# Prompt attention of a decoder trunk: quads of heads visited in pairs instead of one after another

## What is computed

```python
def sparse_attend(q, k_sel, v_sel, valid):
    s = jnp.einsum('bqhd,bqkhd->bqhk', q, k_sel, ...) * (DSA_HEAD_DIM ** -0.5)
    s = jnp.where(valid[:, :, None, :], s, -jnp.inf)
    p = jax.nn.softmax(s, axis=-1)
    return jnp.einsum('bqhk,bqkhd->bqhd', p.astype(v_sel.dtype), v_sel)
...
def dsa_out(o, g, w_out):
    return (o.reshape(B, L, DSA_WIDTH) * jax.nn.silu(g)) @ w_out
```

## Time and profile before

| | |
|---|---|
| median of 3 executions | 1161.84 us (1157.28 to 1166.62) |
| profiled execution, its own time | 1161.64 us |
| its span on the core | 1159.9 us, 25599 instructions |
| PE busy | 1120.7 us (97%), 10579 matmuls |
| PE weight loads | 979.1 us (84%) |
| DVE busy | 675.2 us (58%) |
| ACT busy | 493.8 us (43%) |
| POOL busy | 381.4 us (33%) |
| mean granted TensorE clock | 0.994 |
| prompt attention, first scores to output projection | 579.96 to 678.25 us |

### The profile page before, as it was taken

The page is one execution under the profiler, slowest core; times in us unless marked ns, Lnnn a source line. Parts: engine busy times, 40 slices in busy tenths (PEclk is TensorE's granted clock), DMA queues, the critical chain, the costliest instruction groups (busy, mean ns, idle before and its releaser), DMA issues. The chain is left out here.

```text
span 1159.9 us, 25599 instructions
## 1 busy us (share of the span) xinstructions
PE 1120.7 (97%) x10579; PEld 979.1 (84%) x10579; DVE 675.2 (58%) x1215; ACT 493.8 (43%) x968; POOL 381.4 (33%) x321
## 2 busy tenths in 40 slices
PE   8999999899999999999999899999999999999897
PEld 6889888899758988879945389999999889888796
DVE  6462255854999789677354546596444362245742
ACT  6542366643433321222353444322453451467643
POOL 5534213243313422114300124353344235312330
PEclk9999999999999999999999999999999999999998
DMA  5335233333315787784699932233220335233212
GB/s 169 101 110 164 91 111 113 125 84 98 117 49 162 245 275 244 269 308 141 225 372 353 341 114 77 72 107 121 88 73 3 110 92 162 92 127 111 93 36 78
DMA packets 127787, 168.81 MB, mean 146 GB/s; under 512 B 20384, under 2 KB 93480, under 8 KB 127663
## 3 DMA queue, kind: packets, MB, share of 16 engines
q1 hardware_dynamic: 115609, 152.59, 39.9%
q10 hardware_dynamic: 12062, 14.59, 3.6%
HBM read 150.70 MB, written 16.81 MB: 144 GB/s over the span
## 5 line engine op out<-in xcount | busy, mean ns | idle before, releaser
L737 POOL TENSOR_TENSOR w_lo<-raw,w_hi 128x512 fp32r<-128x512 f32 (+2 forms) x267 | 359.0, 1375 | 700.5 <-ACT w_hi L1501 700.5
L773 PE MATMUL psum<-h_hi,w_hi 128*128 128x272 f32 x1616 | 472.0, 292 | 6.6 <-DVE h_lo L2425 4.7
L775 PE MATMUL psum<-h_hi,w_lo 128*128 128x272 f32 x1616 | 467.9, 290 | 0.0
L774 PE MATMUL psum<-h_lo,w_hi 128*128 128x272 f32 x1616 | 465.5, 288 | 0.0
L773 PEld LDWEIGHTS psum<-h_hi,w_hi 128*128 128x128 f32 x1616 | 303.6, 188 | 20.2 <-issue 15.3
L774 PEld LDWEIGHTS psum<-h_lo,w_hi 128*128 128x128 f32 x1616 | 304.1, 188 | 0.1
L775 PEld LDWEIGHTS psum<-h_hi,w_lo 128*128 128x128 f32 x1616 | 303.3, 188 | 0.0
L1501 ACT ACTIVATE w_hi<-raw 128x1024 fp32r<-128x1024 f32 (+1 forms) x137 | 135.5, 1034 | 121.9 <-PE psum L775 82.5
L773 PE MATMUL psum<-w_hi,h_hi 128*128 128x512 f32 (+2 forms) x352 | 126.0, 358 | 1.2 <-DVE dsa_score_s L2519 0.8
L775 PE MATMUL psum<-w_hi,h_lo 128*128 128x512 f32 (+2 forms) x352 | 122.3, 347 | 1.6 <-issue 1.6
L774 PE MATMUL psum<-w_lo,h_hi 128*128 128x512 f32 (+2 forms) x352 | 122.7, 349 | 1.0 <-issue 1.0
(11 more groups left out here) (331 smaller groups left out, 1385.5 us busy)
## 6 DMA issues: line engine op xcount, KB each, us to landing
smp_keys<-in_cache_k_dram SPq DMA_DIRECT2D x128, 256.0 KB, 4.7
raw<-in_gla_w_in_dram SPq DMA_DIRECT2D x23, 1024.0 KB, 5.4
spare<-in_cache_v_dram SPq DMA_DIRECT2D x36, 512.0 KB, 6.4
raw<-in_dsa_w_in_dram SPq DMA_DIRECT2D x17, 1024.0 KB, 5.3
raw<-in_cache_v_dram SPq DMA_DIRECT2D x28, 512.0 KB, 6.7
gla_s_in<-in_state_gla_dram SPq DMA_DIRECT2D x16, 512.0 KB, 8.0
raw<-in_gla_w_out_dram SPq DMA_DIRECT2D x8, 1024.0 KB, 6.7
out_dram<-gla_s_in ACTq DMA_DIRECT2D x16, 512.0 KB, 4.6
```

The lines of the kernel that those rows point to most:

```text
L737: pool.tensor_tensor(copies(key, pair_view(w_lo, key)[:, k]), raw_copies(key, k), copies(key, pair_view(w_hi, key)[:, k].bitcast(F32)), AL ...
L773: pe.matmul(out, lh, rh, start=start, stop=False)
L774: pe.matmul(out, lh, rl, start=False, stop=False)
L775: return pe.matmul(out, ll, rh, start=False, stop=stop)
```

## The change

`QUADS` gets another order, and the quads are taken in pairs whose units alternate: tile 3 with tile 0 (first half of the heads), tile 2 with tile 1 (first half), tile 2 with tile 1 (second half), and at the end tile 0 with tile 3 (second half), the last four units being tile 0, 0, 3, 3. `QUAD_OF[n]` is the quad of unit n, `FIRST_OF` and `LAST_OF` are the first and last unit of each quad (0, 1, 8, 9, 16, 17, 24, 25 and 6, 7, 14, 15, 22, 23, 29, 31). Two quads now fill banks 4 and 5 at once. The branches of two paired quads stand in neighbouring iterations: 10 and 11, 18 and 19, 26 and 27, then 33 and 35. The work, the sizes and the number of instructions are the same; the list of tiles by unit is

| unit n | 0-3 | 4-7 | 8-11 | 12-15 | 16-19 | 20-23 | 24-27 | 28-31 |
|---|---|---|---|---|---|---|---|---|
| tile before | 2 2 2 2 | 3 3 3 3 | 1 1 1 1 | 2 2 2 2 | 1 1 1 1 | 0 0 0 0 | 0 0 0 0 | 3 3 3 3 |
| tile after | 3 0 3 0 | 3 0 3 0 | 2 1 2 1 | 2 1 2 1 | 2 1 2 1 | 2 1 2 1 | 0 3 0 3 | 0 0 3 3 |

```diff
--- before.py
+++ after.py
@@ -77,8 +77,11 @@
 
 PAIR_AREA = (0, 1, 0, 1, 0, 1, 0, 1, 0, 1, 0, 1, 0, 1, 1, 1)
 
-QUADS = [(2, 0), (3, 0), (1, 0), (2, 1), (1, 1), (0, 0), (0, 1), (3, 1)]
-UNITS = [(t, 4 * half + h) for t, half in QUADS for h in range(4)]
+QUADS = [(3, 0), (0, 0), (2, 0), (1, 0), (2, 1), (1, 1), (0, 1), (3, 1)]
+QUAD_OF = [2 * p + y for p in range(3) for _ in range(4) for y in range(2)] + [6, 7, 6, 7, 6, 6, 7, 7]
+UNITS = [(QUADS[m][0], 4 * QUADS[m][1] + QUAD_OF[:n].count(m)) for n, m in enumerate(QUAD_OF)]
+FIRST_OF = [QUAD_OF.index(m) for m in range(8)]
+LAST_OF = [max(n for n in range(32) if QUAD_OF[n] == m) for m in range(8)]
 
 OUT_PIECES = [(t, half) for half in range(2) for t in range(3)] + [(3, 0), (3, 1), (SMP, 1)]
 
@@ -1384,9 +1387,9 @@
 
                 def values_of(n):
                     t, h = units[n]
-                    m = n // 4
+                    m = QUAD_OF[n]
                     b = 4 + m % 2
-                    if n % 4 == 0:
+                    if n == FIRST_OF[m]:
                         claim(b, ("O", L, m), ("oT_read", L, t, h // 4))
                     pe.wait_ge(*on("PT_read", L, n))
                     for s in range(t + 1):
@@ -1958,7 +1961,7 @@
                         .then_inc(*sig("PT_read", L, n))
 
                 def branch_hi(m):
-                    t, h = units[4 * m]
+                    t, h = units[FIRST_OF[m]]
                     act.wait_ge(*on("oT_read", L, t, h // 4))
                     copy(H[L % 2][0][:, h:h + 4, cols(t)], tmp_d[:].rearrange("p (k t) -> p k t", k=4))\
                         .then_inc(*sig("h_hi", (L, "out"), t, h // 4))
@@ -1985,8 +1988,8 @@
                                        accum_out=ast[:, n % 3, 2:3]).then_inc(*sig("p_exp", L, n))
                     if 2 <= n <= len(units) + 1:
                         pt_out(n - 2)
-                    if n >= 7 and n % 4 == 3:
-                        branch_hi((n - 7) // 4)
+                    if n - 4 in LAST_OF:
+                        branch_hi(LAST_OF.index(n - 4))
                     if n == 2 + last_spare[0][2] // 2 * 2:
                         split_hi(pair_of[(L, "out", 0)])
                 split_hi(pair_of[(L, "out", 1)])
@@ -2617,10 +2620,10 @@
                     dve.tensor_scalar(x, x, ast[:, n % 3, 3:4], None, ALU.mult).then_inc(*sig("p_norm", L, n))
 
                 def branch(m):
-                    t, h = units[4 * m]
-                    dve.wait_ge(*on("O", L, 4 * m + 3))
+                    t, h = units[FIRST_OF[m]]
+                    dve.wait_ge(*on("O", L, LAST_OF[m]))
                     if m:
-                        pt, ph = units[4 * m - 4]
+                        pt, ph = units[FIRST_OF[m - 1]]
                         dve.wait_ge(*on("h_lo", (L, "out"), pt, ph // 4))
                     dve.tensor_tensor(tmp_d[:].rearrange("p (k t) -> p k t", k=4),
                                       psum[:, 4 + m % 2, :].rearrange("p (k t) -> p k t", k=4),
@@ -2638,8 +2641,8 @@
                         shift(n)
                     if 1 <= n <= len(units):
                         normalise(n - 1)
-                    if n >= 7 and n % 4 == 3:
-                        branch((n - 7) // 4)
+                    if n - 4 in LAST_OF:
+                        branch(LAST_OF.index(n - 4))
                 dve.wait_ge(*on("h_hi", (L, "out"), SMP, 1))
                 hi, lo = H[L % 2]
                 dve.tensor_tensor(lo[:, :, SEQ:TOK], tmp_d2[:].rearrange("p (h t) -> p h t", h=DH),
```

## The result

The changed kernel takes 1168.17 us (median of 8, 1164.61 to 1171.19), the kernel before 1161.63 us in the same comparison (1157.28 to 1166.62). The ratio is 1.0055, with a 95% interval of 1.0034 to 1.0077: slower by 6.5 us, clear of noise and inside 1%. The forecast was 1168.7. It had also said that a measurement tells about 1% from no change; this comparison resolved 0.55%.

The account below looks back on a forecast made before the run. A chain from even units' scores through PE, DVE, ACT and back to PE was taken to set each pair: 6.75 + 1.3 + 0.45 - 0.6 - 1.0 = +6.9 us on 1161.84 gives 1168.7, likeliest range 1164 to 1174, overall 1158 to 1176.

Parts of the forecast that it names:

- The chain and its parity: Even unit's scores through DVE and ACT to PE's value page set each pair of iterations; large even units cost +6.75 us.
- The 11 pairs: Iteration pairs beginning at units 2 to 12 and 18 to 26, over which the chain's +6.75 us was summed.
- pair 26: Iterations from scores 26 to scores 28: PE's own work sets them, 0.45 us more than the chain, so +0.45 us.
- Neighbouring branches: Two adjacent branches on DVE delay shifts 12 and 20, 0.7 us late at unit 12: +1.3 us, bounds 0 and 4.
- Pairs 0, 14, 16: Iteration pairs beginning at units 0, 14 and 16 lose a few blocks, 0.1 to 0.3 us each: -0.6 us.
- Pair 28: Scores 28 to scores 30: normalise 27 ends 4.2 us after scores 28, the pair takes 8.75 instead of 9.75: -1.0 us.
- The end: Scores 30 to output projection: single transposes and a later branch, 9.7 us against 9.79, so 0.
- The clock rival: Holes in the four tile 3 and 0 pairs lower PE's clock, 1.7 us each: 1175.5 us; chance 0.09.
- PE's work as the pace: Rival: PE's work paces the pairs, so tile 3 units fill tile 0's holes: 1157.8 us; chance 0.13.

Follow-up runs that it names:

- Experiment 1: Changed kernel with the two quads of each of the first three pairs exchanged, so the small unit is even: 1159.54 us, ratio 0.9981 to the kernel before.
- Experiment 2: Changed kernel with the new order of quads but each quad done alone, not alternated: 1160.20 us, ratio 0.9993 to the kernel before.
- Experiment 4: Changed kernel with the first branch of each of the first three pairs one iteration earlier on DVE and ACT: 1165.27 us, ratio 1.0032.
- experiment 6: Changed kernel with ACT's split of the first output weights in iteration 29 instead of 26, so POOL's low part later too: 1166.57 us, ratio 1.0040.
- experiment 3: Changed kernel with ACT's copy for unit n-2 ahead of exponential n instead of behind it: 1163.55 us, ratio 1.0010.
- experiment 5: Kernel before the change, with ACT's copy for unit n-2 ahead of exponential n: 1159.24 us, ratio 0.9977.
- experiment 8: Changed kernel with small unit even, copy ahead of exponential, first branch of a pair earlier and weight split in iteration 29: 1156.33 us, ratio 0.9959.
- first kernel of experiment 9: Changed kernel loading only half of each cached value page (output partly wrong): executed once, 1171.2 us.
- experiment 7: Changed kernel with the small unit on the even place and the output weights' split in iteration 29: 1157.56 us, ratio 0.9962.
- second kernel of experiment 9: Kernel of experiment 8 loading only half of each cached value page (output partly wrong): 1151.05 us, ratio 0.9926.

## Why the prediction was right

The forecast was +6.9 us, all of it in the stage. The medians of the whole kernel differ by 6.5 us. In the profiled executions the stage alone grew by 8.5.

- **The chain and its parity** was right, in mechanism and size. The 11 pairs together moved by 66.82 - 58.72 = +8.1 us; the forecast for them, with the branches and pair 26, was 6.75 + 1.3 + 0.45 = 8.5. The numbers put down to look for were 6.6 for the pairs of tiles 3 and 0 (6.53 to 6.59), 3.7 from the even scores to values of tile 3 (3.58) and 5.8 for pairs 18 and 22 (5.81, 5.75). Experiments 1 and 2 show that parity is the cause.
- **Neighbouring branches**: the right mechanism, its size 0.9 us (2 x 0.47) instead of 1.3. Experiment 4 took exactly that away at units 12 and 20.
- **Pairs 0, 14, 16**: -0.5 against -0.6. **Pair 26**: 4.60 against 4.63 (4.18 + 0.45).
- **Pair 28** is the step that failed: "8.75, -1.0" became 11.35, +1.6. Two things were missing. DVE's durations were taken from rows in which POOL was idle; with POOL at work they grew, and normalise 27 ended 5.05 us behind scores 28 instead of 4.2. The trace of before had shown it: its low part at 660.66, beside POOL's work, took 0.99 us and not 0.69 (last section). And PE's wait grew with it to 2.19 us, behind which the clock fell for one value page: 3.52 - 1.85 = 1.67 us.
- **The end**: 9.08 us against "I get 9.7", -0.7 against 0. Which of the two opposite effects, single transposes and a later branch, was mis-sized was not tested by itself.
- **The clock rival** came true once, but not as I had put it. The holes of 0.64 to 0.86 us, two in each of pairs 2, 4 and 6, did not move the clock: it was 1.00 through all the pairs of the stage up to 670 us. It fell behind one wait of 2.19 us. I had weighed the rule of the Trainium skill ("TensorE: Matmul & The Clock Gate", "A second HAM failure mode: psum-queue depth-cycling") as one price on four pairs. No fall followed the short and frequent idling in this trace; the one fall in the stage stands behind a single longer wait.

The stage's misses (+2.6 at pair 28, +0.1 at pairs 0, 14 and 16, -0.4 at the branches, -0.7 at the end) add up to the 1.6 us between 6.9 and 8.5. Without the 1.67 us of the clock's fall the stage grew by 6.8 us. So the mechanism earned the sign and most of the size, but that 1168.7 lies only 0.5 us from the median of 1168.17 is partly luck: the misses cancel, and the clock decides how many of them an execution shows. That the medians differ by 6.5 and not by 8.5 fits the clock, whose falls differ from execution to execution by 1.7 us or more each; how often pair 28 has one in executions without a profile stays open.

PE's work as the pace (1157.8) was nearly the picture of another kernel: with the small unit even the same alternation took 1159.54, with some waits left in it.

## What to carry to other kernels

In a software pipeline over engines that take their queues in order, look for the one chain that is not covered by other work, and ask which element of each group stands at its head (here the even unit). Alternating large and small units helps where the small one heads the chain and hurts where the large one does: the same edit was 0.5% slower in one parity and 0.2% faster in the other. And put a copy that others wait for ahead of the long operation that nobody waits for yet.

## What the runs showed of the hardware

- **POOL slows DVE.** With POOL at work on tiles in SBUF, in the change, DVE's subtraction of two SBUF tiles of 128x512 took 1.58 us instead of 0.69, and its multiplication by a scalar 0.84 instead of 0.49 (512 columns) and 0.70 instead of 0.29 (128 columns); a product with one input in PSUM kept 0.68. Moving POOL's work restored all of them (experiment 6). How much it costs depends on the moment. In experiment 4 the multiplication of 128 columns took 1.36 us. In the kernel before, beside the same work of POOL (658.60 to 664.03), the subtraction took 0.99 and neither multiplication was slower:

```profile
660.66 0.99 DVE L2217 TENSOR_TENSOR h_lo<-dsa_tmp,h_hi 128x512 fp32r<-128x512 f32 x1 [3.28 <-ACT h_hi L1501]
...
662.62 0.28 DVE L2617 TENSOR_SCALAR att_p<-att_p,dsa_ast 128x128 f32<-128x128 f32 x1
...
663.87 0.49 DVE L2617 TENSOR_SCALAR att_p<-att_p,dsa_ast 128x512 f32<-128x512 f32 x1
```

  POOL's work is four instructions, and the slowed rows end shortly behind one of them. These are the third and the fourth in the change (each row from a window of its own):

```profile
666.68 1.27 POOL L740 TENSOR_TENSOR w_lo<-raw,w_hi 128x512 fp32r<-128x512 f32 x1
...
667.90 1.72 POOL L740 TENSOR_TENSOR w_lo<-raw,w_hi 128x512 fp32r<-128x512 f32 x1
```

  The subtraction ended at 668.50, 0.55 us behind the third; the multiplication of 512 columns at 669.91, 0.29 behind the fourth. In the kernel before the subtraction ended at 661.65, 0.54 behind POOL's second (661.11). So DVE seems to have waited until POOL's instruction was through. That is read from rows, and not tested. The Trainium skill ("SBUF — State Buffer", "Who interferes with whom") states that a DVE instruction with two SBUF inputs contends with a GpSimd instruction that reads SBUF, that one in a mode that uses both ports contends with GpSimd, and that one with at most one SBUF input outside those modes doesn't. The subtraction and the product agree with it in every row here; that the multiplications ran in such a mode no row shows.
- **The clock and one wait of PE.** In the stage, PE waits of 2.19 us in the change, 2.20 in experiments 1 and 4, 2.43 in experiment 3, 2.01 in experiment 5, 2.44 in experiment 8 and 2.20 in the first kernel of experiment 9 each went with a fall of the clock to the lower level, within the wait or within 0.8 us of its end, for a stretch between 3 us and 14 us. Where no wait of the stage was longer than 1.58 us (the kernel before, experiments 2, 6 and 7, the second kernel of experiment 9) it stayed 1.00. The length of the wait is not all of it: near 508 us PE idled 2.08 us in experiment 7 and 2.15 in the second kernel of experiment 9 and the clock stayed 1.00 (505 to 515 us), and the falls of the kernel before at 51 and 925 us have no such wait ahead of them. What else decides stays open. In the change the wait and the slow page together cost 2.19 + 1.67 = 3.9 us; in experiment 3, pair 28 and the end took 24.9 us, against 17.9 in experiment 6.
